# Another order of the 64 experts in a mixture-of-experts loop, and one expert fewer with a fixed place

## The reference

```python
idx, gates = route(xf, w_router, router_bias)     # 8 of 64 experts per token
def expert_block(args):
    tok, e = args
    xb = xpad[tok]
    hb = jax.nn.silu(xb @ w_gate[e]) * (xb @ w_up[e])   # 1024 -> 256, twice
    return hb @ w_down[e]                                # 256 -> 1024
...
shared = (jax.nn.silu(xf @ ws_gate) * (xf @ ws_up)) @ ws_down
return (routed + shared).reshape(B, T, D)
```

## Time and profile before

| what | us |
|---|---|
| time, median of 3 runs | 1075.47 (1075.21 to 1076.78) |
| the profiled execution, own time | 1077.48 |
| its span | 1075.65 |
| first gate/up of the loop starts | 409.00 |
| last result of the loop is copied out | 1001.70 |
| span of the loop | 592.7 |

### The profile page before, as it was taken

The page is one execution under the profiler, slowest core; times in us unless marked ns, Lnnn a source line. Parts: engine busy times, 40 slices in busy tenths (PEclk is TensorE's granted clock), DMA queues, the critical chain, the costliest instruction groups (busy, mean ns, idle before and its releaser), DMA issues.

```text
span 1075.6 us, 17979 instructions
## 1 busy us (share of the span) xinstructions
PE 1002.1 (93%) x7100; PEld 449.5 (42%) x7100; DVE 326.3 (30%) x815; ACT 227.1 (21%) x537; POOL 160.9 (15%) x232
## 2 busy tenths in 40 slices
PE   6999999999999999999999999899898999899474
PEld 2655556565455554333443333333332343333121
DVE  0122226764236773111121111111111121111177
ACT  1211105664123231111121111111111121111011
POOL 1000010300221121211212211211111112110000
PEclk9999999999999999999999999999999999999798
DMA  9954419400400756699999999999999999994596
GB/s 371 406 238 173 157 31 247 165 1 1 176 40 31 270 213 241 230 387 405 390 421 422 420 420 420 421 419 416 421 418 414 408 420 421 419 416 186 236 410 261
DMA packets 59676, 321.64 MB, mean 299 GB/s; under 512 B 9748, under 2 KB 10396, under 8 KB 31560
## 3 DMA queue, kind: packets, MB, share of 16 engines
q1 hardware_dynamic: 43184, 272.71, 63.2%
q0 software_dynamic: 14240, 43.34, 10.3%
q10 hardware_dynamic: 2168, 4.43, 1.1%
HBM read 298.78 MB, written 31.39 MB: 307 GB/s over the span
## 4 chain that ended last, share of the span: by engine, by line
PE 75%; DMA 15%; DVE 5%; ACT 2%; issue 1%; SPq 1%; POOL 0%; POOLq 0%; DVEq 0%; ACTq 0%
PE bank L1977 27%; PE bank L1997 13%; PE bank L1571 8%; DMA ring<-in_w_up 8%; PE bank L1742 5%; PE bank L1949 3%; DMA ring<-expert_rows 3%; DMA reg_p<-in_w_up 3%; PE bank L1836 3%; PE bank L1598 2%; PE bank L1769 2%; PE bank L1560 2%; PE bank L1849 2%; PE bank L1755 1%; PE bank L1842 1%
## 5 line engine op out<-in xcount | busy, mean ns | idle before, releaser
L1977 PE MATMUL bank<-ring,reg_h 128*32 128x512 f32 x2528 | 330.9, 601 | 14.1 <-DMA ring<-in_w_up 12.3
L1977 PEld LDWEIGHTS bank<-ring,reg_h 128*32 128x32 f32 x2528 | 98.6, 111 | 200.3 <-issue 200.2
L1997 PE MATMUL bank<-ring,reg_y 128*32 128x512 f32 x1264 | 166.9, 594 | 1.5 <-ACT reg_y L997 1.5
L1977 PE MATMUL bank<-reg_p,reg_h 128*32 128x512 f32 x608 | 128.5, 601 | 2.0 <-DMA ring<-in_w_up 2.0
L1443 DVE TENSOR_TENSOR reg_h<-reg_p,bank 128x256 f32<-128x256 f32 x49 | 20.6, 421 | 342.3 <-ACT reg_p L1015 300.5
L707 POOL DMA_INDIRECT expert_rows<-reg_y,rowc x49 | 49.2, 1003 | 259.4 <-DVE reg_y L1427 258.1
L1015 ACT ACTIVATE reg_p<-bank 128x256 f32<-128x256 f32 x49 | 18.8, 383 | 327.2 <-PE bank L1977 327.2
L1571 PE MATMUL bank<-ring,reg_h 128*128 128x384 f32 (+2 forms) x256 | 84.3, 487 | 0.0
L1997 PEld LDWEIGHTS bank<-ring,reg_y 128*32 128x32 f32 x1264 | 46.2, 110 | 82.7 <-issue 78.7
L1427 DVE TENSOR_SCALAR reg_y<-bank,reg_p 128x512 f32<-128x512 f32 x49 | 36.8, 751 | 138.3 <-PE bank L1997 138.3
L1742 PE MATMUL bank<-ring,reg_h 128*128 128x512 f32 x160 | 70.3, 594 | 0.0
(11 more groups left out here) (272 smaller groups left out, 967.3 us busy)
## 6 DMA issues: line engine op xcount, KB each, us to landing
ring<-in_w_gate SPq DMA_DIRECT2D x51, 1024.0 KB, 15.2
ring<-in_w_up SPq DMA_DIRECT2D x51, 1024.0 KB, 21.4
ring<-in_w_down SPq DMA_DIRECT2D x51, 1024.0 KB, 20.0
ring<-in_w_mod SPq DMA_DIRECT2D x21, 1024.0 KB, 8.0
ring<-expert_rows SPq DMA_DIRECT2D x19, 1024.0 KB, 14.2
reg_p<-in_w_gate SPq DMA_DIRECT2D x13, 1024.0 KB, 14.0
reg_p<-in_w_up SPq DMA_DIRECT2D x13, 1024.0 KB, 22.8
reg_p<-in_w_down SPq DMA_DIRECT2D x13, 1024.0 KB, 21.9
```

The costliest lines, as they stand in the source:

```text
L1977: last = pe.matmul(bank[2 + p][R * j:R * j + R, :], xg_t[:, p, k * P + R * j:k * P + R * j + R], w_gu(homes[n % SLOTS])[:, k], start=(k == ...
L1997: last = pe.matmul(bank[5 + hf][R * j:R * j + R, :], h_t[:, p, i * P + R * j:i * P + R * j + R], w_dn(homes[n % SLOTS])[:, i, 512 * hf:512 ...
```

## The change

Four things change.

- `FIXED` is 1: only expert 0 has a known place. Expert 1 is ranked by its count like the others, so its rank, its place and its home aren't known before the counts are.
- `UNITS` has one 4 less, one 3 more, one 2 more, and no 1. The sum is 196 as before, and there are 49 blocks as before.
- `ORDER` isn't "fullest, emptiest, second fullest, ..." any more. `expert_order` picks at each place the rank that brings the sum of units nearest to a line `due`: the mean of the units times the place, less up to 8 units (`BEHIND`) at first, plus up to 6 (`AHEAD`) later, with both fading towards the ends (`EDGE`).
- SyncE doesn't load place 1 ahead of `s_eid`. It reads the four expert numbers of places 1 to 4, then loads places 1 and 2 in full; from place 3 on its program is as before.

```diff
--- before.py
+++ after.py
@@ -46,9 +46,27 @@
 NEG = -1e30
 ROUTED = 2.5
 R = 32
-FIXED = 2
-UNITS = (4,) * FIXED + (5,) * 5 + (4,) * 15 + (3,) * 20 + (2,) * 21 + (1,)
-ORDER = tuple(range(FIXED)) + tuple(FIXED + (i // 2 if i % 2 == 0 else E - FIXED - 1 - i // 2) for i in range(E - FIXED))
+FIXED = 1
+UNITS = (4,) * FIXED + (5,) * 5 + (4,) * 15 + (3,) * 21 + (2,) * 22
+EDGE, BEHIND, AHEAD = 8, 8, 6
+
+
+def expert_order():
+
+    left, total = list(range(FIXED, E)), 0
+    count, mean = len(left), sum(UNITS[FIXED:]) / len(left)
+    order = list(range(FIXED))
+    for n in range(1, count + 1):
+        x = n / count
+        due = mean * n - BEHIND * min(1, n / EDGE) * (1 - x) + AHEAD * x * min(1, (count - n) / EDGE)
+        r = min(left, key=lambda rank: (abs(total + UNITS[rank] - due), UNITS[rank]))
+        left.remove(r)
+        order.append(r)
+        total += UNITS[r]
+    return tuple(order)
+
+
+ORDER = expert_order()
 FIRST = tuple(sum(UNITS[r] for r in ORDER[:n]) for n in range(E))
 TILES = tuple((n, u) for n, r in enumerate(ORDER) for u in range(UNITS[r]))
 NQ = len(TILES) // 4
@@ -579,12 +597,11 @@
             sp.wait_ge(s_op, 2 * T)
             sp.wait_ge(s_x2, 2 * T)
             sp.wait_ge(s_h2a, T)
-            load_gate_up(1, 1)
-            load_down(1, 1)
             sp.wait_ge(s_eid, 1)
-            e = {n: sp.value_load(eid[0:1, n:n + 1], min_val=0, max_val=E - 1) for n in (2, 3, 4)}
-            load_gate_up(2, e[2])
-            load_down(2, e[2])
+            e = {n: sp.value_load(eid[0:1, n:n + 1], min_val=0, max_val=E - 1) for n in range(FIXED, SLOTS)}
+            for n in (1, 2):
+                load_gate_up(n, e[n])
+                load_down(n, e[n])
             sp.wait_ge(s_shg, T - 1)
             load_gate_up(3, e[3])
             sp.wait_ge(s_shg, T)
```

## The result

The changed kernel takes 1065.41 us (median of 4 executions, 1063.73 to 1068.04), the kernel before 1076.12 us beside it; the ratio is 0.9901, with a 95% interval of 0.9876 to 0.9926. The same kernel in five more rounds took 1064.82 us, ratio 0.9880 (0.9858 to 0.9902). So it is faster by some 11 to 12 us. The forecast was 1060.5 us (15.0 us less) in a range of 1054 to 1068.5.

A forecast was written before the change was run, and what follows sets the result against it. Weights (DMA) were short for most of the loop, PE's beat close behind. Waits and slow matmuls of 23.0 us fall to 8.0, gaining 15.0: 1077.48 to 1062.5, less 2.0 to the median, 1060.5 us; range 1054 to 1068.5.

The forecast's parts named there:

- Place 1 behind the list: cost 0: Before the loop: place 1's three later loads take 7.5 us of the 10.5 us free from 366 to 400; cost 0.
- The loop starts at 409: Block 0: its gather, beside the moved loads, is late by between 0 and 5 us, taken as 0.
- Place 7 at about 430, the next load at 439.5, the share from 435 to 446 above 0.6: Early loop: block 1 releases place 7's home, so the queue restarts at 439.5 with 22 loads issued, not 446.25 with 20.
- PE's beat and the floor of 1052.5: Whole loop: PE needs 11.6 us a block; if it never waits, 23.0 us are gained, giving 1052.5.
- Waits fall from 16.2 to between 5 and 9: PE's gate/up waits in the loop: from 16.2 us to 5 to 9; largest lateness 6.3 us.
- the one slow stretch of 1.7 us: Behind the last wait: one block's matmuls run slow for 1.7 us, making 8.0 us with the 6.3 of lateness.
- Where they are: Lateness by place: 3.3 us to spare at place 9, 0.3 at 13; late by 5.6 at 59, 6.3 at 63.
- the supply line: Landing times of up loads: 3.26 us a load from 439.5 up to place 32, then 9.20 us an expert.
- My check: The line laid against PE's need in the kernel before: latest by 24.4 us, where the trace lost 23.0.
- rival 2: The start starves: PE waits 5 to 8 us around block 8 and again at the end, 1066 to 1070; chance 0.16.
- A lead of 13.3 us for every later load: Loads behind the queue's restart: 6.75 us earlier restart plus two loads of 3.26 us put every later load 13.3 us ahead.

The follow-up runs named there:

- the second profile: The changed kernel once more, unaltered, in five rounds against the kernel before: 1064.82 us, ratio 0.9880; loop 581.7 us.
- the gentler line: The changed kernel with EDGE, BEHIND, AHEAD = 4, 6, 4 instead of 8, 8, 6: 1059.20 us, ratio 0.9835 against the kernel before.

## Why the prediction was right, and where it was off

The time was inside the range, and the direction and the main mechanism (place 7's home is free earlier, and the queue doesn't run dry) were as forecast. The 1060.5 was 4.3 to 4.9 us too low. About 1 us of that is the point from which it counts: it took the profiled execution of the kernel before to lie 2.0 us above the median, by three times, but with more executions that median is 1076.1 to 1077.6, and the execution (1077.48) lies near it. The rest, 3 to 4.3 us, is a smaller gain than 15.0. Step by step:

- *Place 1 behind the list: cost 0.* Right, shown both ways. The gap from 366 to 400 took the loads, as worked out from the earlier trace rows.
- *The loop starts at 409.* Right (408.84): the gather of block 0 wasn't late.
- *Place 7 at about 430, the next load at 439.5, the share from 435 to 446 above 0.6.* Right: 429.86, 439.08, 0.99. That this is the main source was shown by holding it back: the loop is 10 to 12 us longer, for a forecast lead of 13.3.
- *PE's beat and the floor of 1052.5.* Right: 1052.18 with half of the up loads.
- *Waits fall from 16.2 to between 5 and 9.* Right: 8.3, though in part by luck, as the next point shows. With the slow matmuls I had 8.0 us in all and it was 9.9, so the gain in the loop was 13.3 for 15.0. In the second profile it was 11.0: the one slow stretch of 1.7 us was two there, 4.2 us.
- *Where they are.* Half wrong. I had place 9 with 3.3 us to spare and place 13 with 0.3, and the largest lateness at place 63 in block 48. In fact place 9's up landed at 463.9 where the line said 459.1, place 19's at 560.6 for 556.9, place 59's at 936.8 for 932.2. The term that was mis-sized is the supply line. It puts these loads 2 to 5 us too early (place 13's up landed at 500.3 for 498.2), and the one that counts, place 59, was some 10 us late against a PE that never waits, for 5.6. In the middle it errs the other way: by the landings in the trace the ups of places 24 to 40 were there 2 to 4 us before it. My check was of the total alone, 24.4 for 23.0. Place by place the line doesn't fit the kernel before either: place 10's up landed at 485.8 (issued at 469.9, 15.9 on the way) where the line has 482.1, place 19's at 573.1 for 570.1, place 24's at 619.7 for 619.0. It joins two points, the restart of the queue at 446.25 and the landing at 697.1, and the loads between them aren't evenly spaced. Why they aren't is open. The last wait, which I had near 963 to 972 in block 48, was at 936.96 in block 45. Part of rival 2 (PE waits at block 5 and 8) came true at 1.8 to 3.9 us, where I priced it at 5 to 8.
- *"A lead of 13.3 us for every later load."* Wrong as a rule. By the landings in both traces it was 12.1 at place 9, 16.4 at place 32 (697.1 and 680.7) and 6.7 at place 59, which landed at 943.5 before (issued at 921.4, 22.1 on the way) and at 936.8. From 900 to 966 the DMA share had fallen to 0.94 where it had been 1.01 before. I had said that the queue stays full behind 440; towards the end it doesn't.

That PE's late wait hangs on the order of the last places was shown by moving one expert (it went from block 45 to 48) and by the gentler line (it went nearly away); that it hangs on bytes too was shown by half of the late up loads. What the two have in common can be read from the traces. A place's load can't go out before its home is free, so what counts is the number of blocks from the one that frees the home to the one that wants it. Place 59's home is free at 907.06, at the end of block 42; its up goes out 5.0 us later, behind down of place 57 in SyncE's order, and takes 24.7 us, 29.7 in all; PE is ready for it at 933.70, in block 45, 26.6 us after the release. In the kernel before this distance is 3 or 4 blocks at every place, in the changed kernel 2 at places 6, 9 and 60. Every wait for gate and up in the 14 profiles is at a place with a distance of 2 or 3, none at one with more. The prediction's reckoning has no such term; it set the landings by bytes alone.

## What to carry to other kernels

Where a loop is bound by weights for one part and by the engine for another, look for the stretch in which the DMA queue is dry because the homes are full: the order of unequal work decides when homes are released. Small pieces first fill that stretch, and cost a wait where a place is wanted so soon after its home is free that the load can't be there. So write out for each place how many blocks lie between the two, beside the sum of bytes; here a milder slope at both ends did better than a steep one. What takes a wait away early also brings the engine sooner to every later place, so it doesn't take away a late wait as well. Check a supply line against the trace place by place, not only in its total.

## What the runs showed of the hardware

- What runs ahead of the loop, the same but for place 1's loads, reached it between 406.5 and 409.7 us in 14 profiles. A spread of 3 us between executions is thus there before the part that is studied, and the length of a stage is a better measure than the whole when a few us matter.
- Waits of nearly the same length differ in what follows them. In the kernel before, the matmuls behind a wait of 1.99 us (852.60) ran partly at the lower clock, and those behind one of 2.90 (927.10) did not the earlier trace rows; in the changed kernel it followed 3.09 us (560.71) and not 3.26 (936.96). In the 14 profiles together, of 20 waits for weights of 3.09 us and more 19 were followed by slow matmuls in the same block, which cost 1.3 to 2.9 us; of the 8 between 1.99 and 2.90 us four were, at 1.5 to 1.7 us; of the 24 shorter ones none. An estimate of a kernel like this should price them by that, and not at 1.7 us for one wait in all.
- DMA throughput at a share of 1.0 isn't one number: 422 GB/s from 450 to 500 us after the change, 403 in the same stretch before.
